# First pair's rows selected on chip by TensorE products, and two weight units asked for behind the second pair's gather

## The chip, the cores and the metric

The kernel runs on one core of one Trainium2 chip. The metric is the device time of one execution in microseconds (us). The kernel before takes 1109.01 us, the median of three runs (1107.18 to 1111.49). Besides its compute engines (PE for matrix products, DVE, ACT and POOL) the core has SP, which here only issues transfers, and 16 DMA engines which all issuing engines share.

## The reference

It is a decoder trunk with two layers over 512 tokens of 1024 f32 values. The first layer mixes tokens by differential attention, the second by multi-head latent attention. Each is followed by a mixture of experts: 4 groups of 8 experts, of which a token uses the best two of its best group. All weights are f32. What matters here:

```python
def hier_moe(h, w_group, b_group, w_router, b_router, w1, w3, w2):
    ...
    g_idx = jnp.argmax(g_prob + b_group.astype(jnp.float32), axis=-1)
    ...
    _, e_idx = lax.top_k(e_prob + b_router.astype(jnp.float32)[g_idx], TOP_K)
    ...
        a = jnp.einsum('nd,edf->nef', t, w1[g])
        b = jnp.einsum('nd,edf->nef', t, w3[g])
        hid = jax.nn.silu(a) * b * combine[:, g, :, None]
        out = out + jnp.einsum('nef,efd->nd', hid, w2[g])
```

with w1 and w3 of shape (1024, 256) and w2 of shape (256, 1024) for each of the 32 experts.

## The kernel before

The change lies in the experts of both layers. The 32 experts are taken as 16 pairs, expert n with expert n + 16. A pair's tile has 128 rows: the first 64 are tokens of expert n, the last 64 tokens of expert n + 16. Tokens beyond 64 of one expert go to overflow tiles, behind the ninth pair.

**Routing.** `gate(l)` on DVE finds the two experts of each token (`OH`, one-hot, and `Mb`, their sum). `route(l)` on PE (line 918) counts, by products with a triangle and with ones, the rank of each token within its expert. DVE turns the ranks into places in the pair's tile (`place`, lines 2040 to 2044) and those into the one-hot `hot_place` (line 2047). PE multiplies it with `hot_token` (line 936), which gives, for all 16 pairs at once, the token number of each place. DVE writes these to `idx` (line 2052).

**Rows of a pair.** The normed rows `XN` were written to HBM (`xn_d`) before. POOL waits for `idx` and gathers the rows of pair 0 into `xg[0]` and of pair 1 into `xg[1]`, by two indirect transfers (line 2515, semaphores gath0 and gath1). PE turns `xg[0]` (`turn_first_pair`, line 969), and ACT and DVE scale it into `xgT` (`modulate_first_pair`). While nothing is to be done, PE runs `keep_busy`, products on a unit matrix whose result nobody reads (line 741).

**A step.** `expert_step(l, n)` on PE: `into_hidden` for w1 (semaphore a) and for w3 (b), both at line 979; the turn of the next pair's rows (951) and of the hidden values (986); `out_of_hidden` for w2 (y, line 994). In step 0 the place table of all pairs is made between b and the turn (`weigh_places`, line 945), from one-hots that DVE made in `weigh(l)` (lines 2077 to 2095). DVE reads it in `tables_out`, and POOL scatters the results of each pair to `y_d` (line 2529).

**The weights.** A step needs six units of 1 MB: two of w1, two of w3, two of w2. SP asks for units in a fixed order (line 565). There are 22 places for units: six in `ring`, six each in the regions RQK and AHS, two in `X` (18 and 19, "the residual's place"), two in `spare`. The first 22 units of a layer are asked for as their places come free; two of these, number 8 and 9 (w3 of pair 1), go into `X`, and SP asks for them last, behind this wait:

```python
for b in range(2):
    sp.wait_ge(sem(f"gath{b}"), 16 * (PAIRS // 2 * l + 1))
first_units(l, 18, 19)
experts(l, BANKS, (4, 5))
```

Each further unit, from number 22 on, waits for the step that read its place 22 units before: those for w1 places for a, for w3 places b, for w2 places y. SP handles all in order, so all of them also stand behind the wait above.

Of the kernel before, what the change touches and what calls it, by code (L numbers as in the profile page):

```python
# [30 lines left out]
P = 128  # L31
# [36 lines left out]
BANKS = 3  # L68
SLOTS = BANKS * RING + 4
# [160 lines left out]
def build(nc, A, out):  # L230
    stack = ExitStack()
    with stack:
# [6 lines left out]

        def sem(name):  # L240
# [160 lines left out]
        half_of, place, over_cap, raw = scratch(PS, 2 * T), scratch(PS, 2 * T), scratch(PS, 2 * T), scratch(PS, 2 * T)  # L401
# [12 lines left out]
        hotp = view(GM, 0, 2 * T, P)  # L414

# [82 lines left out]
        def _(sp):  # L498
# [89 lines left out]
            for l in range(2):  # L588
# [16 lines left out]
                for b in range(2):  # L605
                    sp.wait_ge(sem(f"gath{b}"), 16 * (PAIRS // 2 * l + 1))
# [44 lines left out]
        def _(pe):  # L651
# [266 lines left out]
            def route(l):  # L918

                pe.wait_ge(sem("el"), 2 * (l + 1))  # L920
                keep_busy(3, 16)
                pe.wait_ge(sem("M"), l + 1)
                ranks = PB[6][:, 0:T * E].rearrange("p (t e) -> p t e", t=T)
                mm(PB[6][:, 0:T * E], trib[:, :], Mb.rearrange("p t e -> p (t e)"), start=True, stop=False)
# [30 lines left out]
            def turn_pair(l, n, chunks):  # L955

                b, m = n % 2, PAIRS * l + n
                pe.wait_ge(sem(f"gath{b}"), 16 * (PAIRS // 2 * l + n // 2 + 1))
# [54 lines left out]
            def expert_step(l, n):  # L1013
# [13 lines left out]
                if n == 0:  # L1027
                    pe.wait_ge(sem("xhA"), l + 1)
                    pe.wait_ge(sem("xhD"), l + 1)
# [11 lines left out]
                if n == 0:  # L1041
                    weigh_places(l)
# [15 lines left out]
                out_of_hidden(w, tiles).then_inc(sem("y"), 1)  # L1058

# [239 lines left out]
        def _(act):  # L1299
# [329 lines left out]
            def modulate_first_pair(l):  # L1629

                for h, (turned, done) in enumerate((("xh", "xhA"), ("xgt", "xA"))):
# [93 lines left out]
        def _(dve):  # L1725
# [262 lines left out]
            def gate(l):  # L1988
# [46 lines left out]
                tt(hot_step, oh[:, :, 0:PAIRS], oh[:, :, PAIRS:], ALU.add)  # L2035
                link(red(half_of, oh[:, :, PAIRS:], AX.X, ALU.add))
                tt(hot_token, hot_step, over(token_v.rearrange("p t k -> p (t k)"), 2, PAIRS), ALU.mult)
                link(ts(half_of, half_of, float(CAP), None, ALU.mult))
# [3 lines left out]
                ts(over_cap, raw, CAP - 0.5, 1024.0, ALU.is_ge, ALU.mult)  # L2042
                link(tt(place, raw, half_of, ALU.add))
                link(tt(place, place, over_cap, ALU.add))
                for h in range(2):
                    js = slice(T * h, T * h + T)
                    tt(hot_place[:, js], over(place[:, js], 2, P), over(iota_p, 1, T), ALU.is_equal).then_inc(sem("hotp"), 1)
                dve.wait_ge(sem("rank"), 2 * l + 2)
                link(v.tensor_copy(cnt, PB[7][:, T * E:(T + 1) * E]))
                v.tensor_copy(rank, PB[6][:, 0:T * E].rearrange("p (t e) -> p t e", t=T))  # L2050
                dve.wait_ge(sem("tab"), 2 * l + 1)
                ts(idx[:, 0:PAIRS], PB[2][:, 0:PAIRS], -1.0, float(S), ALU.mult, ALU.add).then_inc(sem("idx"), 1)
# [3 lines left out]
                link(red(extra, cmp, AX.X, ALU.add))  # L2056
                cur = extra
# [15 lines left out]
            def weigh(l):  # L2073
# [13 lines left out]

                link(tt(slots, over(slotf, 2, NPAIR), over(starts, 1, 2 * T), ALU.is_ge))
# [8 lines left out]
            def tables_out(l):  # L2097

                dve.wait_ge(sem("tab"), 2 * l + 2)
# [534 lines left out]
```

## Time and profile before

| | |
|---|---|
| time of the profiled execution | 1109.18 us |
| its span | 1107.4 us |
| granted TensorE clock, mean | 0.988 |
| PE busy | 1041.3 us, 94% of the span |
| DVE busy | 611.5 us, 55% |
| ACT busy | 328.6 us, 30% |
| POOL busy | 92.0 us, 8% |
| HBM read | 320.90 MB |
| chain that ended last, by engine | PE 75%, DMA 10%, DVE 5%, SP's queue 4% |
| experts of the first layer, first product to last step's last product | 350.38 to 551.2 us |
| experts of the second layer, the first product | 862.95 us |

The span is that of the profiled execution, which took 1.8 us more than its span. Times in the rows are in microseconds from the span's start. A busy share of PE does not say that PE sets the time: the products of `keep_busy` count too. What a change in one stage is worth is read from the waits of that stage and of those behind it.

### The profile page before, as it was taken

Reading aid. Unit: us, or ns where it says so; the run is one execution under the profiler, and the core shown is the slowest. Engines: PE = TensorE matmul, PEld = TensorE weight load, DVE = VectorE, ACT = ScalarE, POOL = GpSimd, SP = SyncE. Lnnn points to the kernel's source line nnn. Section 1 sums busy time; section 2 is a strip of 40 time slices with the busy share of each in tenths; the row PEclk is TensorE's granted clock in tenths of the full one; section 3 lists DMA queues with packets and bytes.
Section 4 is the critical chain, followed back from the end, with each engine's and each line's share of the span. In section 5 each row is a group of like instructions: output and inputs, shape, how many; then the busy total and the mean of one; then the engine's idle time right before and its main releaser. Section 6 shows DMA issues by size and latency. Waiting matters only on the chain.

```text
span 1107.4 us, 15314 instructions
## 1 busy us (share of the span) xinstructions
PE 1041.3 (94%) x5662; PEld 630.0 (57%) x5662; DVE 611.5 (55%) x1479; ACT 328.6 (30%) x891; POOL 92.0 (8%) x129
## 2 busy tenths in 40 slices
PE   6999999999998999898889999999998899979986
PEld 5444444555458666565556566565456666646652
DVE  6799989898647422222246577877236622222224
ACT  4321111874231211111114555666122211111110
POOL 1000000000011212121000000000000111101100
PEclk8999999999998999999999999999999999999999
DMA  9939967947578999999996400401837899999998
GB/s 366 404 132 395 393 264 297 386 171 297 235 291 328 401 419 418 418 418 419 417 394 269 166 1 1 189 2 50 367 115 305 346 419 419 417 397 417 419 416 351
DMA packets 66814, 341.44 MB, mean 308 GB/s; under 512 B 11110, under 2 KB 11366, under 8 KB 36400
## 3 DMA queue, kind: packets, MB, share of 16 engines
q1 hardware_dynamic: 49952, 297.68, 66.7%
q0 software_dynamic: 15120, 37.63, 8.9%
q10 hardware_dynamic: 1664, 5.09, 1.2%
q8 instruction: 48, 0.79, 0.3%
q14 instruction: 30, 0.25, 0.1%
HBM read 320.90 MB, written 37.24 MB: 323 GB/s over the span
## 4 chain that ended last, share of the span: by engine, by line
PE 75%; DMA 10%; DVE 5%; SPq 4%; ACT 3%; issue 3%; ACTq 0%; DVEq 0%; POOLq 0%
PE PP L979 16%; PE PP L732 12%; PE PP L842 10%; PE PP L994 8%; DMA AHS<-in_moe_w 5%; SPq L565 4%; PE PP L754 3%; PE PP L1199 3%; PE PP L1165 2%; PE PP L1203 2%; DMA AHS<-y_d 2%; PE PP L802 2%; PE PP L705 2%; PE PP L791 2%; PE PP L951 1%
## 5 line engine op out<-in xcount | busy, mean ns | idle before, releaser
L732 PE MATMUL PP<-ring,AHS 128*128 128x512 f32 x320 | 139.9, 592 | 0.0
L2148 DVE TENSOR_TENSOR PS<-PS,PP 128x256 f32<-128x256 f32 x33 | 13.9, 421 | 193.2 <-PE PP L979 183.7
L842 PE MATMUL PP<-ring,AHS 128*128 128x512 f32 x256 | 112.2, 594 | 0.0
L732 PEld LDWEIGHTS PP<-ring,AHS 128*128 128x128 f32 x320 | 59.7, 190 | 69.8 <-issue 69.8
L2155 DVE SCALAR_TENSOR_TENSOR PS<-PP,small,GF 128x512 f32<-128x512 f32 x66 | 46.5, 747 | 95.8 <-PE PP L994 85.4
L842 PEld LDWEIGHTS PP<-ring,AHS 128*128 128x128 f32 x256 | 47.8, 190 | 56.9 <-issue 56.9
L1642 ACT ACTIVATE PS<-PP 128x256 f32<-128x256 f32 x33 | 12.6, 383 | 216.5 <-PE PP L979 186.8
L979 PE MATMUL PP<-RQK,RV 128*64 128x256 f32 x640 | 71.9, 379 | 2.7 <-issue 2.7
L979 PE MATMUL PP<-AHS,RV 128*64 128x256 f32 (+1 forms) x592 | 68.7, 380 | 2.3 <-DVE RV L2142 1.3
L979 PE MATMUL PP<-ring,RV 128*64 128x256 f32 (+1 forms) x528 | 64.3, 391 | 4.1 <-issue 2.1
L979 PEld LDWEIGHTS PP<-RQK,RV 128*64 128x64 f32 x640 | 54.7, 137 | 21.9 <-issue 8.9
L979 PEld LDWEIGHTS PP<-AHS,RV 128*64 128x64 f32 (+1 forms) x592 | 51.1, 138 | 19.5 <-issue 6.6
L979 PEld LDWEIGHTS PP<-ring,RV 128*64 128x64 f32 (+1 forms) x528 | 49.1, 144 | 20.7 <-issue 8.7
L2529 POOL DMA_INDIRECT y_d<-PS,row x31 | 31.8, 1027 | 329.0 <-DVE PS L2155 286.1
L1872 DVE TENSOR_REDUCE small<-PP 128x2 f32<-128x256 f32 (+3 forms) x64 | 52.5, 822 | 8.5 <-PE PP L757 8.4
L2124 DVE TENSOR_SCALAR RV<-PP,small 128x128 f32<-128x128 f32 x124 | 42.4, 406 | 24.1 <-PE PP L951 23.2
L1748 DVE SCALAR_TENSOR_TENSOR ring<-ring,PS 128x1024 f32<-128x1024 f32 x44 | 51.8, 1221 | 4.3 <-DMA ring<-in_ada_t 3.9
L1646 ACT ACTIVATE PS<-PP 128x256 f32<-128x256 f32 x33 | 12.6, 383 | 136.4 <-PE PP L986 136.4
L1618 ACT ACTIVATE RV<-PP,small 128x128 f32<-128x128 f32 x124 | 46.6, 456 | 3.5 <-PE PP L951 3.5
L741 PE MATMUL PP<-ident 128*128 128x128 f32 x280 | 40.3, 307 | 4.4 <-POOL GM L2435 2.2
L1429 ACT ACTIVATE AHS<-PP,small 128x256 f32<-128x256 f32 (+3 forms) x82 | 41.1, 510 | 11.0 <-DVE small L1872 10.8
L1748 DVE SCALAR_TENSOR_TENSOR AHS<-AHS,PS 128x1024 f32<-128x1024 f32 x36 | 42.5, 1222 | 1.5 <-DMA AHS<-in_ada_t 1.0
(366 smaller groups left out, 1711.4 us busy)
## 6 DMA issues: line engine op xcount, KB each, us to landing
AHS<-in_moe_w SPq DMA_DIRECT2D x54, 1024.0 KB, 23.0
RQK<-in_moe_w SPq DMA_DIRECT2D x52, 1024.0 KB
ring<-in_moe_w SPq DMA_DIRECT2D x49, 1024.0 KB, 21.9
ring<-in_ada_t SPq DMA_DIRECT2D x22, 1024.0 KB, 21.1
AHS<-in_ada_t SPq DMA_DIRECT2D x18, 1024.0 KB
spare<-in_moe_w SPq DMA_DIRECT2D x16, 1024.0 KB, 13.6
X<-in_moe_w SPq DMA_DIRECT2D x16, 1024.0 KB
ring<-in_da_w_qkv SPq DMA_DIRECT2D x10, 1024.0 KB, 13.3
```

What stands on the lines that cost most here:

```text
L565: sp.dma_start(unit(slot), (w1, w3, w2)[k // 2][l][n + PAIRS * (k % 2)]).then_inc(s_w[slot], 16)
L732: last = mm(PB[qkv_bank(n)][:, :], HT[:, c, t * P:(t + 1) * P], us[c // 4][:, (c % 4) * NH:(c % 4 + 1) * NH], start=c == 0, stop=c == C - 1)
L741: mm(PB[bank][:, 0:P], ident[:, :], ident[:, :], start=True, stop=True)
L842: last = mm(PB[2 * t + n][:, :], (OT, OTM)[l][:, k, t * P:(t + 1) * P], us[k // 2][:, (k % 2) * D + n * NH:(k % 2) * D + (n + 1) * NH], st ...
L979: last = mm(o[s0:s1, 0:FF], xgT[b][:, c, s0:s1], w(2 * m + e)[:, c * FF:(c + 1) * FF], start=c == 0, stop=c == C - 1)
L994: last = mm(PB[5 + m][s0:s1, :], hidT[:, c, s0:s1], w(4 + e)[:, c * D + m * NH:c * D + (m + 1) * NH], start=c == 0, stop=c == 1)
L1429: last = fn(dst, src, ACT.Exp, bias=nmx[:, b, a:a + 1], accum_out=total)
L1618: last = fn(xgT[b][:, c, :], PB[0][:, (c // 2) * P:(c // 2 + 1) * P], ACT.Identity, bias=MODC[:, l, 3 + V_SHIFT, c:c + 1], scale=GC[:, 2 * ...
L1748: last = stt(wt, wt, 1.0, condb, ALU.mult, ALU.mult, accum_out=MODC[:, l, w, 2 * q + c:2 * q + c + 1])
L1872: red(nmx[:, b], o, AX.X, ALU.max, negate=True).then_inc(sem("nm"), 1)
L2124: last = ts(xgT[b][:, c, :], PB[1][:, (c // 2) * P:(c // 2 + 1) * P], GC[:, 2 * l + 1, c:c + 1], MODC[:, l, 3 + V_SHIFT, c:c + 1], ALU.mul ...
L2155: last = stt(ysb[b][:, cols], PB[5 + m][:, :], weight, GF[:, cols], ALU.mult, ALU.mult)
```

## The change

For pair 0 alone the rows no longer come by a gather. DVE makes `take_first`, for each of the four tiles of 128 tokens a one-hot of 128 tokens by 128 places of the tile, in f32; PE multiplies each with that tile's `XN`, two halves of 512 columns by four tiles, and sums them in PSUM; ACT copies one half into `xg[0]`, DVE the other. To tell experts 16 to 31 apart, PE adds 1024 to their ranks by a product of ones with `eights`. The token numbers of all pairs are made behind the products of the rows, so `idx` comes after them. POOL then gathers pair 1 first. SP waits for gath1 alone. `weigh(l)` is split in three; its last part and `weigh_places` move behind the hidden values and behind w2's products of step 0.

```diff
@@ sync
-                for b in range(2):
-                    sp.wait_ge(sem(f"gath{b}"), 16 * (PAIRS // 2 * l + 1))
+                sp.wait_ge(sem("gath1"), gathered(l, 3))
                 first_units(l, 18, 19)
@@ tensor, route
-                keep_busy(3, 16)
+                keep_busy(3, 10)
+                for _ in range(6):
+                    mm(PB[3][:, 0:P], onesb[:, :], onesb[:, :], start=True, stop=True)
+                pe.wait_ge(sem("iota"), 2 * l + 1)
+                ranks = PB[6][:, 0:T * E].rearrange("p (t e) -> p t e", t=T)
+                mm(ranks, onesb[:, :], eights.unsqueeze(1).broadcast_to([P, T, E]), start=True, stop=False)
...
                 keep_busy(3, 5)
+                for _ in range(8):
+                    mm(PB[3][:, 0:P], onesb[:, :], onesb[:, :], start=True, stop=True)
                 for h in range(2):
-                    pe.wait_ge(sem("hotp"), 2 * l + h + 1)
+                    for t in range(T):
+                        if h == 0:
+                            pe.wait_ge(sem("hotp"), 6 * l + t + 1)
+                        last = mm(PB[3 + h][:, :], take_first[:, t], XN[:, t, h * NH:(h + 1) * NH], start=t == 0, stop=t == T - 1)
+                    last.then_inc(sem("tab"), 1)
+                for h in range(2):
+                    pe.wait_ge(sem("hotp"), 6 * l + T + h + 1)
                     for j in range(T * h, T * h + T):
                         last = mm(PB[2][:, 0:PAIRS], hot_place[:, j], hot_token[:, j], start=j == 0, stop=j == 2 * T - 1)
                 last.then_inc(sem("tab"), 1)
-                pe.wait_ge(sem("idx"), 2 * l + 1)
-                keep_busy(3, 16 if l else 22)
@@ tensor, turn_first_pair
-                pe.wait_ge(sem("gath0"), 16 * (PAIRS // 2 * l + 1))
...
+                    if c % (C // 2) == 0:
+                        pe.wait_ge(sem("xhD" if c else "xhA"), 2 * l + 1)
@@ scalar, modulate_first_pair
+                act.wait_ge(sem("tab"), 4 * l + 1)
+                fn(xg[0][:, 0:NH], PB[3][:, :], ACT.Identity).then_inc(sem("xhA"), 1)
@@ vector, gate
+                link(tt(first_at, raw, elsewhere, ALU.add))
+                for t in range(T):
+                    link(ts(take_first[:, t], iota_h, first_at[:, 2 * t:2 * t + 1], None, ALU.is_equal))
+                    stt(take_first[:, t], iota_h, first_at[:, 2 * t + 1:2 * t + 2], take_first[:, t],
+                        ALU.is_equal, ALU.add).then_inc(sem("hotp"), 1)
...
+                dve.wait_ge(sem("tab"), 4 * l + 2)
+                v.tensor_copy(xg[0][:, NH:D], PB[4][:, :]).then_inc(sem("xhD"), 1)
+                dve.wait_ge(sem("tab"), 4 * l + 3)
+                ts(idx[:, 0:PAIRS], PB[2][:, 0:PAIRS], -1.0, float(S), ALU.mult, ALU.add).then_inc(sem("idx"), 1)
@@ gpsimd
-                for n in range(2):
-                    gather_pair(n)
+                gather_pair(1)
```

On PE, in `route` and step 0 of the first layer, the order before is this (741 is `keep_busy`, 936 the token numbers, 969 the turn of pair 0, 979 products into the hidden values, 945 `weigh_places`):

```order
L741 MATMUL PP<-ident 128x128 x5
L936 MATMUL PP<-PS 128x16 x8
L741 MATMUL PP<-ident 128x128 x22
L969 MATMUL PP<-ident,RV 128x128 x8
L979 MATMUL PP<-AHS,RV 64x256 x16
L979 MATMUL PP<-RQK,RV 64x256 x16
L945 MATMUL PP<-PS,GM 128x64 x8
L951 MATMUL PP<-ident,RV 128x128 x5
```

and after it is this (746 and 943 keep PE busy, 948 selects rows, 953 makes the token numbers, 985 turns pair 0, 995 goes into and 1010 out of the hidden values, 960 is `weigh_places`):

```order
L746 MATMUL PP<-ident 128x128 x5
L943 MATMUL PP<-onesb 128x128 x8
L948 MATMUL PP<-RV,GM 128x512 x8
L953 MATMUL PP<-PS 128x16 x8
L985 MATMUL PP<-ident,RV 128x128 x8
L995 MATMUL PP<-AHS,RV 64x256 x16
L995 MATMUL PP<-RQK,RV 64x256 x16
L966 MATMUL PP<-ident,RV 128x128 x5
L1002 MATMUL PP<-ident,PS 128x128 x2
L966 MATMUL PP<-ident,RV 128x128 x3
L1010 MATMUL PP<-RQK,PS 64x512 x8
L960 MATMUL PP<-PS,GM 128x64 x8
```

The 22 idle products are gone, the 8 selecting products of 512 columns stand ahead of the token numbers, and `weigh_places` moved behind w2's products.

On DVE, at the end of `gate` of the first layer, the writing of `idx` stood behind two short copies (2047 makes `hot_place`):

```order
L2044 TENSOR_TENSOR PS<-PS 128x8 [waits s_dve]
L2047 TENSOR_TENSOR PS<-PS 128x512 [waits s_dve]
L2047 TENSOR_TENSOR PS<-PS 128x512
L2049 COPY PS<-PP 128x32 [waits s_rank]
L2050 COPY PS<-PP 128x128 [waits s_dve]
L2052 TENSOR_SCALAR idx<-PP 128x16 [waits s_tab]
```

and now it stands behind the copy of half of pair 0's rows, which itself waits for the second half of the selecting products:

```order
L2070 COPY PS<-PP 128x32 [waits s_rank]
L2071 SCALAR_TENSOR_TENSOR PS<-PS,PP 128x128 [waits s_dve]
L2073 TENSOR_TENSOR PS<-PS,small 128x128
L2074 TENSOR_REDUCE PS<-PS 128x32 [waits s_dve]
L2077 COPY RV<-PP 128x512 [waits s_tab,s_xd,s_dve]
L2079 TENSOR_SCALAR idx<-PP 128x16 [waits s_tab]
L2172 TENSOR_SCALAR RV<-PP,small 128x128 [waits s_xh,s_gf]
```

What moved is `idx`, for which POOL's gather of pair 1 waits, and behind that SP.

## Rows read from the trace of the kernel before

**Rows 1.** The page's slices of the span, DMA share in tenths

```profile
DMA  9939967947578999999996400401837899999998
```

**Rows 2.** Chain that ended last, in order of time: start us, us, what

```profile
340.17 1.29 DVE PS L2047 x2
...
357.51 1.93 PE PP L945 x16
...
517.65 29.84 DMA AHS<-in_moe_w
...
856.82 4.32 DMA RV<-xn_d,idx
...
1039.68 29.54 DMA AHS<-in_moe_w
```

**Rows 3.** Waits of PE, stretch 470 to 552 us: us in total, times, longest us

```profile
PE PP L979 <- issue: 4.1, 3, 2.1
...
PE PP L994 <- DMA ring<-in_moe_w: 1.1, 1, 1.1
...
PE PP L994 <- DMA AHS<-in_moe_w: 0.6, 1, 0.6
```

**Rows 4.** SP's queue in order of time: start us, us, line, operation

```profile
332.49 0.83 SPq L565 DMA_DIRECT2D AHS<-in_moe_w  x2
...
348.28 0.80 SPq L565 DMA_DIRECT2D X<-in_moe_w  x2
...
354.09 1.95 SPq L565 DMA_DIRECT2D AHS<-in_moe_w  x2
...
862.92 0.80 SPq L565 DMA_DIRECT2D X<-in_moe_w  x2
...
992.11 0.33 SPq L565 DMA_DIRECT2D ring<-in_moe_w  x1
```

**Rows 5.** Busy time by stretch: us, engines, PEclk, DMA share, GB/s

```profile
343.00:348.00 5.00, 5.00 (x32) 5.00 (x32) 3.44 (x16) 0.00 (x0) 2.07 (x2) 0.66 0.46 128
...
882.00:902.00 20.00, 19.30 (x144) 12.14 (x142) 5.84 (x16) 4.05 (x11) 3.24 (x4) 1.00 1.01 416
...
991.00:995.00 4.00, 1.73 (x11) 0.80 (x11) 1.47 (x3) 0.00 (x0) 0.73 (x1) 1.00 0.77 266
```

**Rows 6.** Timeline of the second layer: start us, us, engine, line

```profile
853.99 1.29 DVE L2047 TENSOR_TENSOR PS<-PS 128x512 f16<-128x512 f32 x2
...
855.64 0.17 DVE L2052 TENSOR_SCALAR idx<-PP 128x16 int32<-128x16 f32 x1
...
856.82 1.05 POOL L2515 DMA_INDIRECT RV<-xn_d,idx  x1 [13.73 <-issue]
...
858.18 1.03 POOL L2515 DMA_INDIRECT RV<-xn_d,idx  x1 [0.30 <-issue]
...
861.19 1.09 PE L969 MATMUL PP<-ident,RV 128*128 128x128 f32 x8 [1.49 <-DMA RV<-xn_d,idx]
...
862.95 3.67 PE L979 MATMUL PP<-AHS,RV 128*64 128x256 f32 x32 [0.66 <-DVE RV L2142]
```

**Rows 7.** Timeline of the first layer, the same places

```profile
342.04 6.80 PE L741 MATMUL PP<-ident 128*128 128x128 f32 x44 [0.27 <-DVE idx L2052]
...
344.35 1.02 POOL L2515 DMA_INDIRECT RV<-xn_d,idx  x1 [0.30 <-issue]
...
348.69 1.04 PE L969 MATMUL PP<-ident,RV 128*128 128x128 f32 x8
...
350.38 3.67 PE L979 MATMUL PP<-AHS,RV 128*64 128x256 f32 x32 [0.66 <-DVE RV L2142]
...
357.55 0.42 DVE L2148 TENSOR_TENSOR PS<-PS,PP 128x256 f32<-128x256 f32 x1 [0.70 <-PE PP L979]
```

**Rows 8.** Chain that ended last: products of 512 columns

```profile
309.56 13.82 PE PP L842 x32
```

**Rows 9.** DMA queues in the stretch 340 to 560 us: packets, MB, share

```profile
q0 software_dynamic: 4647, 8.15, 10.1%
```

More of the change, by code:

```diff
@@ L68 @@
 BANKS = 3
+HALF = 1024
 SLOTS = BANKS * RING + 4
@@ L238, in build, with gathered @@
         sems = {}
+        def gathered(l, n):
+            return 16 * ((PAIRS // 2 - 1 + n % 2) * l + (n - 1) // 2)
         def sem(name):
@@ L400, in build @@
         hot_step, hot_token = scratch(PS, 2 * T, PAIRS), scratch(PS, 2 * T, PAIRS, dt=F16)
-        half_of, place, over_cap, raw = scratch(PS, 2 * T), scratch(PS, 2 * T), scratch(PS, 2 * T), scratch(PS, 2 * T)
+        raw, iota_h, eights = scratch(PS, 2 * T), scratch(PS, P, dt=F16), scratch(PS, E, dt=BF16)
+        elsewhere, first_at = scratch(PS, 2 * T), scratch(PS, 2 * T)
         assert at[0] <= 2816
@@ L414, in build @@
         hotp = view(GM, 0, 2 * T, P)
+        take_first = view(GM, 0, T, P)
         def probabilities(i, a):
@@ L1058, in expert_step @@
                 out_of_hidden(w, tiles).then_inc(sem("y"), 1)
+                if n == 0:
+                    weigh_places(l)
             def overflow_tile(l, i, b):
@@ L2041, in gate @@
                 link(red(raw, slots, AX.X, ALU.add))
[L2042 to L2047, printed above, removed]
+                link(tt(first_at, raw, elsewhere, ALU.add))
[3 more added lines that the diff above has]
+                        ALU.is_equal, ALU.add).then_inc(sem("hotp"), 1)
+                for j in range(2 * T):
+                    last = ts(hot_place[:, j], iota_h, raw[:, j:j + 1], None, ALU.is_equal)
+                    if j % T == T - 1:
+                        last.then_inc(sem("hotp"), 1)
                 dve.wait_ge(sem("rank"), 2 * l + 2)
                 link(v.tensor_copy(cnt, PB[7][:, T * E:(T + 1) * E]))
-                v.tensor_copy(rank, PB[6][:, 0:T * E].rearrange("p (t e) -> p t e", t=T))
-                dve.wait_ge(sem("tab"), 2 * l + 1)
-                ts(idx[:, 0:PAIRS], PB[2][:, 0:PAIRS], -1.0, float(S), ALU.mult, ALU.add).then_inc(sem("idx"), 1)
+                stt(rank, over(eights, 1, T), -float(P), PB[6][:, 0:T * E].rearrange("p (t e) -> p t e", t=T), ALU.mult, ALU.add)
                 cmp = masked.rearrange("p t e -> p (t e)").rearrange("p (e k) -> p e k", k=LEVELS)
@@ L2071, in gate, with weights @@
                 link(red(slotf, slots, AX.X, ALU.add))
-            def weigh(l):
+            def weights(l):
                 slots = picked.rearrange("p t k e -> p (t k) e")
@@ L2086, in weigh @@
                 link(tt(Wt, Wt, over(s1, 2, 2), ALU.mult))
+            def weigh(l):
+                slots = picked.rearrange("p t k e -> p (t k) e")
                 link(tt(slots, over(slotf, 2, NPAIR), over(starts, 1, 2 * T), ALU.is_ge))
@@ L2165, in expert_step @@
                 if n == 0:
-                    tables_out(l)
+                    weigh(l)
                 if n < LAST:
@@ L2171, in expert_step @@
                     spread(hot_last, tokf[:, n:n + 1])
+                if n == 0:
+                    tables_out(l)
                 dve.wait_ge(sem("y"), m + 1)
@@ L2203, in experts @@
                 modulate_first_pair(l)
-                weigh(l)
+                overflow_places(l)
+                weights(l)
                 for n in range(BETWEEN):
@@ L2483, in tables @@
                            channel_multiplier=0, allow_small_or_imprecise_dtypes=True)
+                    g.iota(iota_h.rearrange("p (a b c d) -> p a b c d", a=2, b=2, c=8), [[HALF, 2], [32, 2], [1, 8], [8, 4]],
+                           base=0, channel_multiplier=0, allow_small_or_imprecise_dtypes=True)
+                    g.iota(eights, [[HALF // P, 2], [0, PAIRS]], base=0, channel_multiplier=0, allow_small_or_imprecise_dtypes=True)
                     g.iota(starts, [[P, NPAIR]], base=0, channel_multiplier=0, allow_small_or_imprecise_dtypes=True)
@@ L2520, in gather_pair @@
                     if n < PAIRS:
-                        b, q = n % 2, PAIRS // 2 * l + n // 2
+                        b = n % 2
                         wait(pool, sem("xgt"), PAIRS * l + n - 1 if n >= 2 else 0)
-                        wait(pool, sem(f"gath{b}"), 16 * q)
+                        wait(pool, sem(f"gath{b}"), gathered(l, n))
                         gather(xg[b], idx[:, n:n + 1], sem(f"gath{b}"))
```

22 lines of the change are left out of this document (11 added, 11 removed).

## The prediction

> **What bounds the kernel now.** I first read the slices of the page [rows 1]. The DMA engines work at nine tenths or more from about 360 us to the end of the first layer's experts, and again in the second layer's; at 882 to 902 us they move 416 GB/s with a share of 1.01 [rows 5], which I take as full. The chain of waits agrees: near the end of both layers' experts it goes through a weight unit that landed 29.84 and 29.54 us after it was asked for [rows 2]. That is a queue, not a latency: a unit of 1.05 MB takes 2.5 us at 416 GB/s. Then the waits of PE: from 470 us to the end of the first layer's experts they add up to 4.1 + 1.1 + 0.6 = 5.8 us, in five short pieces [rows 3]. So PE starts with 22 units in store, eats the store, and late in the experts gets its weights just as they land. From there on only one thing counts: when the DMA engines began their unbroken run, and how much they had to carry.
>
> Next, where that run begins. SP asks for the last units of the store at 332.49 us, then nothing until 348.28 us, when both gathers have landed; then two units for X, and the next at 354.09 us, when step 0 has freed a place [rows 4]. Between 343 and 348 us the DMA engines are at 0.46 and move 128 GB/s [rows 5], which is the two gathers. In the second layer SP goes on at 862.92 us [rows 4]. These two holes are the places where this change can give or cost time. PE's own start counts less, since its steps run ahead of the DMA engines only to wait later.
>
> **PE's start, in the second layer.** Before: `hot_place` runs from 853.99 us, `idx` is written at 855.64, the gathers are issued at 856.82 and 858.18, PE turns the rows from 861.19 and begins step 0 at 862.95 [rows 6].
>
> After: the small DVE work ahead is about the same, and the one-hot of the first tile (two operations of 128 columns, where `hot_place` takes 0.65 us for 512) should be ready near 854.1. PE then does 8 selecting products of 512 f32 columns. The row of the same shape has 32 instructions in 13.82 us [rows 8], and there one product is two instructions, so 8 products are 16 instructions: 16 x 13.82 / 32 = 6.9 us, to 861.0. The one-hots of the other tiles come faster than 0.86 us each and don't hold it up. Then the 8 narrow products for the token numbers: `weigh_places` takes 1.93 us for 8 of 64 f32 columns [rows 2], these have 16 columns of f16, so a quarter or less; I take 0.4 us, to 861.4. ACT's copy of the first half lies under the second half's products; DVE's copy of the second half, of the size of `hot_place`, so 0.7 us, lies under the narrow products and the first four turns. From the turn's start to step 0 it stays 862.95 - 861.19 = 1.76 us [rows 6]: 863.2. PE starts step 0 0.2 us later than before. The gather that goes and the products that come are worth the same.
>
> **PE's start, in the first layer.** The same chain stands 853.99 - 340.17 = 513.8 us earlier [rows 2, 6], so 349.4 us after the change, against 350.38 before: 1.0 us earlier. The gain is not the gather's: 44 idle instructions took 6.80 us from 342.04 and PE turned the rows only at 348.69 [rows 7], when SP shows that both gathers had landed by 348.28 [rows 4]. Either bound, +0.2 or -1.0 us, is under what PE later waits for its weights.
>
> **SP's release, the term that counts.** `idx` now waits for the selecting products, DVE's copy and the narrow products: 861.0 + 0.7 + 0.05, then the write of 0.17 [rows 6], so ready at 862.0 instead of 855.8. POOL issues 1.0 us after (as 855.81 to 856.82), at 863.0. Gather 1 is now the first, so it doesn't stand 1.4 us behind another. Its time to land I take from the first gather of this layer, 4.32 us from its issue [rows 2]; the bounds are 3.93 (344.35 to 348.28, first layer [rows 4, 7]) and 4.74 (858.18 to 862.92 [rows 4, 6]). SP is released at 863.0 + 4.4 = 867.4 in the second layer, 4.5 us later than 862.92, and at 867.4 - 513.8 = 353.6 in the first, 5.3 us later than 348.28. With the bounds: 4.1 to 4.9, and 4.9 to 5.7.
>
> The Trainium skill, page "DMA: Bandwidth & Descriptors", section "Anatomy of one DMA — SWDGE (gpsimd) path", fits such a DMA as 2.0 us plus its bytes over 436 GB/s. For the mean 0.26 MB that would be 2.6 us behind POOL's 1.05 us, 3.7 us in all. The row's 4.32 us is more, and I go by it; by the page each release would be 0.7 us earlier and the time about 1.4 us less.
>
> All this time the DMA engines have nothing but gather 1: the store is full, and unit 22, which could start on a place freed by a (about 353 and 867 us), stands in SP's queue behind the same wait. So the hole grows by the whole delay. What comes off: gather 2 is issued at about its old time, behind gather 1, and now runs in the hole. The gathers and scatters are 8.15 MB in 32 transfers, 10.1% of 220 us, so 0.7 us each [rows 9]: -0.7 us per layer.
>
> **Does the delay reach the end?** In the first layer I see no later hole, the share stays full to the end [rows 1], and PE already waits [rows 3]: +5.3 - 0.7 = +4.6 us, and PE's 1.0 us is only a longer wait. In the second layer there is an overflow tile; SP waits for it until 992.11 [rows 4] and the DMA engines run dry: 991 to 995 us move 266 GB/s [rows 5]. That lacks 4 x (416 - 266) / 416 = 1.4 us of work, which a later queue fills: +4.5 - 0.7 - 1.4 = +2.4 us. Bounds for a layer's passing on: nothing, if DMA has slack I don't see, to all of it, 4.6 + 3.8.
>
> **The other edits.** `weigh_places` (1.93 us) moves behind w2's products: PE has the same work in step 0, 0. Behind it stand `tables_out` and the first scatter, needed many microseconds later. DVE's places and weights now run after the first pair's scaling; DVE stood 0.70 us waiting before the hidden values of step 0 [rows 7] and moves the last part of `weigh` behind them, so I cost it at 0; without that cover it is some tenths in step 0, again under PE's later waits. Pair 1's rows are turned when both products into the hidden values are through, 349.4 + 2 x 3.67 = 356.7 us [rows 7], three microseconds after gather 1 lands. Units 8 and 9 (w3 of pair 1) are read a step later than those of pair 0, and land about 1 + 2 x 2.5 us behind SP's release, near 360, before step 1 has even begun. The shorter `keep_busy`, the product with `eights`, two iotas on POOL while it idles: 0.
>
> **Sum.** 1109.18 + 4.6 + 2.4 = 1116.2 us for an execution like the profiled one; that execution is 0.17 us above the median of the runs, so 1116.0.
>
> **Rivals.**
> 1. *PE's start decides.* If the DMA engines had at least 5 us in hand before the first step that waits for weights, the longer hole would cost nothing, and the steps would end -1.0 + 0.2 us from before: 1108.2, not slower. For it: PE is 94% busy, and the waits of 5.8 us are spread thin. Against it: there are such waits in the first layer, and the share is full before them. It decides only where the delay is smaller than that reserve, and a reserve and waits don't go together.
> 2. *Only one layer passes it on.* In the second layer PE waits less, and the dry stretch may swallow more than its own 1.4 us: 1109.0 + 4.6 = 1113.6.
> 4. *Faster.* It needs 5.5 us, and nothing in the profile has them: even selecting products at half their price would bring SP's release only 3.5 us forward, still later than before.
>
> **How the numbers follow.** Both layers pass the delay on, my forecast: 0.56, own range 1113.5 to 1118.5. One layer alone: 0.18. The clock: 0.12. PE's start: 0.09. Something faster: 0.05. A measurement of this kernel can tell about 0.5%, 5.5 us, from no change, so slower means above 1114.6: all of the clock case and most of the forecast, with a little of the second, 0.66. Within 0.5%: 0.29. The range goes from 1110.5, which leaves out PE's start, to 1119.
>
> **What would show it.** In the changed kernel's profile SP's units into X are asked for near 353.6 and 867.4 us, with the DMA engines all but idle from 343 us and 855 us; 16 instructions of the selecting products take 6.9 us; step 0 begins near 349.4 and 863.2; the waits of PE for weights in the last steps of the first layer grow from about 6 to 11 us. I am wrong if SP is released by 350 us, or if it is late and the last product of the first layer's experts still ends near 551 us.

## The result, and the profile after

The changed kernel takes 1115.47 us (median of 4 runs, 1115.2 to 1115.99), the kernel before 1108.91 (4 runs, 1107.18 to 1111.49): a ratio of 1.0061, interval 1.0045 to 1.0077. It is slower by 6.6 us; the forecast was 1116.0. The profiled execution took 1115.3 us, its span 1113.5, against 1107.4 before, so the traces below differ by 6.1 us.

The page's slices of the changed kernel, DMA share in tenths, to set beside [rows 1]:

```profile
DMA  9939977947586999999996400401847799999998
```

Thirteenth slice: 6 in place of 8. That slice holds the hole in which the DMA engines wait for SP. Its queue in the changed kernel (start us, us, line, operation), beside [rows 4]:

```profile
332.44 0.81 SPq L571 DMA_DIRECT2D AHS<-in_moe_w  x2
353.10 0.80 SPq L571 DMA_DIRECT2D X<-in_moe_w  x2
...
870.75 0.81 SPq L571 DMA_DIRECT2D X<-in_moe_w  x2
```

The stretches of [rows 5] in the changed kernel, with one more (us, engines, PEclk, DMA share, GB/s):

```profile
343.00:348.00 5.00, 5.00 (x23) 2.37 (x21) 1.61 (x7) 0.60 (x1) 0.00 (x0) 1.00 0.01 5
348.00:353.00 5.00, 4.56 (x41) 3.53 (x42) 4.58 (x23) 2.99 (x6) 2.12 (x2) 1.00 0.29 71
...
991.00:995.00 4.00, 2.69 (x7) 0.90 (x5) 1.27 (x2) 0.00 (x0) 0.00 (x0) 1.00 1.00 414
996.00:1007.00 11.00, 5.24 (x26) 3.31 (x28) 0.00 (x0) 0.00 (x0) 2.56 (x3) 0.54 1.01 415
```

SP's next units come 4.8 us later in the first layer (353.10 against 348.28), and ten microseconds go by with the DMA engines nearly idle: 5 GB/s, then 71. The clock is full where the selecting products run. At 991 to 995 us the dry stretch is gone (414 GB/s, 266 before). From 996 to 1007 PE is busy for only 5.24 of 11 us, which I had not forecast.

The changed kernel's timeline, both layers (start us, us, engine, line; 948 selects the rows, 953 makes the token numbers, 2079 writes `idx`, 2551 gathers, 995 goes into the hidden values), beside [rows 6, 7]:

```profile
340.29 7.13 PE L948 MATMUL PP<-RV,GM 128*128 128x512 f32 x16 [0.35 <-DVE GM L2063]
347.26 0.35 PE L953 MATMUL PP<-PS 128*128 128x16 f16 x8
348.16 0.17 DVE L2079 TENSOR_SCALAR idx<-PP 128x16 int32<-128x16 f32 x1
349.20 2.60 PE L995 MATMUL PP<-AHS,RV 128*64 128x256 f32 x22 [0.24 <-DVE RV L2172]
349.29 1.09 POOL L2551 DMA_INDIRECT RV<-xn_d,idx  x1 [19.65 <-PE PP L985]
...
864.71 0.17 DVE L2079 TENSOR_SCALAR idx<-PP 128x16 int32<-128x16 f32 x1
865.74 3.67 PE L995 MATMUL PP<-AHS,RV 128*64 128x256 f32 x32 [0.24 <-DVE RV L2172]
865.88 1.05 POOL L2551 DMA_INDIRECT RV<-xn_d,idx  x1 [20.19 <-PE PP L985]
```

From the first selecting product to the first narrow one is 347.26 - 340.29 = 6.97 us. Everything here is as it was forecast, within half a microsecond. The end of the first layer's experts, before and then after (start us, us, engine, line):

```profile
552.59 7.13 PE L979 MATMUL PP<-RQK,RV 128*64 128x256 f32 x64 [1.35 <-issue]
...
564.22 1.94 PE L1009 MATMUL PP<-RQK,PS 128*64 128x512 f32 x8 [0.55 <-DMA RQK<-in_moe_w]
...
567.66 3.70 PE L1084 MATMUL PP<-PS,RQK 128*128 128x512 f32 x8 [0.19 <-DVE PS L2155]
```

```profile
555.19 7.13 PE L995 MATMUL PP<-RQK,RV 128*64 128x256 f32 x64 [1.34 <-issue]
...
566.87 1.94 PE L1025 MATMUL PP<-RQK,PS 128*64 128x512 f32 x8 [0.56 <-DMA RQK<-in_moe_w]
...
570.31 1.12 PE L1100 MATMUL PP<-PS,RQK 128*128 128x512 f32 x2 [0.19 <-DVE PS L2185]
```

These rows also mend an error: the time table ahead of the prediction, and its last part, call 551.2 us the end of the first layer's experts. That is the end of w2 of the 15th step; the 16th begins at 552.59 and its w2 ends at 566.2. The right comparison is 566.2 against 568.8 us: +2.6.

PE's waits over the last steps of that layer, 470 to 569 us (us in total, times, longest), before:

```profile
PE PP L979 <- issue: 5.4, 4, 2.1
PE PP L1009 <- DMA RQK<-in_moe_w: 1.6, 2, 1.1
PE PP L994 <- DMA ring<-in_moe_w: 1.1, 1, 1.1
...
PE PP L994 <- DMA AHS<-in_moe_w: 0.6, 1, 0.6
...
PE PP L994 <- DMA spare<-in_moe_w: 0.5, 1, 0.5
```

and after:

```profile
PE PP L995 <- issue: 8.5, 6, 2.1
PE PP L1010 <- DMA ring<-in_moe_w: 1.7, 1, 1.7
PE PP L1010 <- DMA spare<-in_moe_w: 1.7, 1, 1.7
PE PP L1025 <- DMA RQK<-in_moe_w: 1.7, 2, 1.1
...
PE PP L1010 <- DMA RQK<-in_moe_w: 0.7, 1, 0.7
...
PE PP L1010 <- DMA AHS<-in_moe_w: 0.5, 1, 0.5
```

Sums: 9.2 and 14.8, so +5.6 us. PE started 1.2 us sooner, and lost 1.7 us less to a halved clock in this layer (3.4 before, 1.7 after, by slices of 2.5 us), so 5.6 - 1.2 - 1.7 = +2.7 us at the end: the DMA engines set the end, and what PE gained it spent waiting. I count the waits that the profile calls "issue" as waits for weights. They stand ahead of w1's or w3's products and grew with the others, but their releaser isn't shown.

What the DMA engines moved gives the same by another way (340 to 400 us; before, changed, then two kernels of the next section: before with SP held, and changed without SP's wait):

```profile
340.00:400.00 60.00, 56.50 (x432) 40.65 (x434) 29.27 (x90) 11.65 (x29) 10.73 (x10) 0.97 0.94 369
340.00:400.00 60.00, 57.99 (x408) 36.32 (x410) 31.61 (x103) 12.37 (x30) 9.76 (x9) 1.00 0.85 344
340.00:400.00 60.00, 56.48 (x434) 40.55 (x436) 29.31 (x90) 11.67 (x29) 10.72 (x10) 0.97 0.87 349
340.00:400.00 60.00, 57.91 (x409) 36.31 (x410) 31.70 (x103) 12.37 (x30) 9.73 (x9) 1.00 0.95 380
```

The changed kernel is 25 GB/s x 60 us = 1.5 MB behind the kernel before. Of these 0.31 MB are pair 0's gather, which it no longer carries (2.26 against 1.95 MB on the gathers' queue), so 1.2 MB of weights are missing, or 2.8 us at 416 GB/s; the layer ended 2.6 us later. By the same sum the held kernel is 1.2 MB or 2.9 us behind, and ended 3.1 later; the one without the wait is 0.66 + 0.31 = 0.97 MB or 2.3 us ahead, and ended 2.0 sooner.

Where the second layer's share went shows in the chain of waits behind its overflow tile (start us, us, what), before and then after:

```profile
988.30 3.71 PE PP L994 x8
...
992.04 1.42 DVE PS L2155 x2
993.46 0.81 issue
994.27 8.78 PE PP L979 x63
```

```profile
989.99 3.71 PE PP L1010 x8
...
993.73 1.42 DVE PS L2185 x2
995.15 6.61 issue
1001.76 1.51 PE PP L995 x5
```

A stall of 0.81 us in which PE waits for nothing that the profile shows has become 6.61. With DVE's part, PE stands 2.27 us before and 8.07 after. The page counts 5662 matmul records of PE before and 5624 after.

### The profile page after: what moved, and what is told of

Same layout as the page of the kernel before. It is cut to its first block, busy times and chain, and to the rows that moved or that the text cites. A ratio compares the mean times of both kernels' runs of the same rounds, so it can differ in the third digit from the quotient of the medians.

```text
span 1113.5 us, 15268 instructions
## 1 busy us (share of the span) xinstructions
PE 1042.9 (94%) x5624; PEld 620.0 (56%) x5624; DVE 616.2 (55%) x1503; ACT 330.3 (30%) x893; POOL 91.2 (8%) x131
## 4 chain that ended last, share of the span: by engine, by line
PE 72%; DMA 9%; DVE 8%; SPq 4%; ACT 4%; issue 4%; ACTq 0%; DVEq 0%; POOLq 0%
PE PP L995 17%; PE PP L737 10%; PE PP L847 10%; PE PP L1010 9%; SPq L571 4%; DMA ring<-in_ada_t 3%; DMA AHS<-in_moe_w 3%; PE PP L759 3%; PE PP L1215 3%; PE PP L1181 2%; PE PP L1219 2%; DMA AHS<-y_d 2%; PE PP L807 2%; PE PP L796 2%; PE PP L966 2%
## 5 line engine op out<-in xcount | busy, mean ns | idle before, releaser
L995 PE MATMUL PP<-ring,RV 128*64 128x256 f32 (+1 forms) x528 | 61.1, 379 | 4.5 <-issue 2.6
L995 PEld LDWEIGHTS PP<-ring,RV 128*64 128x64 f32 (+1 forms) x528 | 46.4, 139 | 20.8 <-issue 9.6
L1950 DVE TENSOR_TENSOR PS<-PP,GM 128x512 f32<-128x512 f32 x16 | 11.1, 691 | 51.0 <-PE PP L847 50.8
```

The source lines that it names most:

```text
L995: last = mm(o[s0:s1, 0:FF], xgT[b][:, c, s0:s1], w(2 * m + e)[:, c * FF:(c + 1) * FF], start=c == 0, stop=c == C - 1)
```

## Experiments: when SP is released

The theory is that of the prediction: what counts is when SP may ask for its next units, and not when PE starts. Three kernels test it.

**The changed kernel without SP's wait.** Edit:

```diff
-                sp.wait_ge(sem("gath1"), gathered(l, 3))
                 first_units(l, 18, 19)
```

> The changed kernel, but SP asks for the two units in X without waiting for a gather. Theory H (what costs is the time in which the DMA engines have nothing to carry before step 0 frees a place): the two units are carried in the hole, SP's next unit waits only for step 0's a at about 353 and 870 us, so the DMA engines are 5 us of work further on in each layer; time 1106 to 1109 us. Gather 1 still lands before 357 us. Rival P (what costs is the selecting products on TensorE's path): step 0 starts as in the changed kernel and the time stays at 1115 to 1116.

Measured: 1109.47 us (12 runs), ratio to before 1.0004 (0.9993 to 1.0014). That is half a microsecond above the range expected, and the wait alone is worth 6.0 us; with it gone the change costs nothing. SP asks at 341.49 us, and the last residual products of the first layer start at 565.7 in place of 570.3, and of 567.66 in the kernel before. The stall behind the overflow tile stays, at 8.43 us. So the even time is a sum: 2.0 us won in the first layer, and 3.2 lost from step 0 to the last residual products of the second (228.8 against 225.6 us), with smaller differences elsewhere.

**The kernel before, holding SP for one gather more.** Nothing else of the change is made.

```diff
                 for b in range(2):
-                    sp.wait_ge(sem(f"gath{b}"), 16 * (PAIRS // 2 * l + 1))
+                    sp.wait_ge(sem(f"gath{b}"), 16 * (PAIRS // 2 * l + 2 - b))
```

> The kernel before, but SP waits for the landing of the third gather (pair 2) too before it asks for the two units in X, near 355 us and 868 us; step 0 starts as in the kernel before. Theory H: SP's release is 5 to 7 us late in each layer with nothing else changed, time 1115 to 1120 us. Rival P: TensorE's path is that of the kernel before, time 1109 us within 2 us.

Measured: 1115.49 us (9 runs), ratio 1.0050 (1.0034 to 1.0066): most of the loss, with PE's instructions as they were. SP's queue:

```profile
353.55 0.81 SPq L565 DMA_DIRECT2D X<-in_moe_w  x2
...
871.11 0.80 SPq L565 DMA_DIRECT2D X<-in_moe_w  x2
```

In the first layer that is the release of the changed kernel, and the layer ends 3.1 us later than before (residual products at 570.79). In the second the likeness of 871.11 and 870.75 misleads. This kernel's gathers are issued there 4.8 us later than before (861.65 against 856.82), so its release is late by only 8.2 - 4.8 = 3.4 us of its own, where the changed kernel's is late by 5.2. From step 0 (867.68) to the last residual products it takes 227.7 us, 2.1 more than the 225.6 before. Another 1.6 us passed between the two layers' experts, where the granted clock was 0.76 from 704 to 711 us and 1.00 before; that is not SP's doing. So the late release is enough for 3.1 + 2.1 = 5.2 us, which is most of the loss, and by the first experiment it is also needed.

**The kernel before without SP's waits.**

```diff
-                for b in range(2):
-                    sp.wait_ge(sem(f"gath{b}"), 16 * (PAIRS // 2 * l + 1))
                 first_units(l, 18, 19)
```

> The kernel before, but SP asks for the two units in X without waiting for the gathers. Theory H: the gathers now share the DMA engines with 2 MB, pair 0's rows land 3 to 5 us later, step 0 and its a come as much later, and so does the unbroken run; 1112 to 1117 us. Rival Q (a wait for a gather is always loss): 1104 to 1107 us.

Measured: 1114.3 us (8 runs), ratio 1.0047 (1.003 to 1.0065). An earlier release is no gain there: the units go ahead of the gathers, PE waits for pair 0's rows, and step 0 starts at 352.8 us in place of 350.4 and at 870.4 in place of 863.0. Of the second delay only 1.9 us arise there: the kernel was already 5.6 us late ahead of its route (DVE's last normed tile at 846.04 against 840.48). In the changed kernel pair 0 needs no gather, so its SP can be let go. That is what the selecting products are good for.

## Experiments: the stall behind the overflow tile

Theory J held that something which PE needs for the next step has to come through full DMA engines; its rival was that the stall follows from the place in PE's program.

**Units asked for later.** The changed kernel, with three units of the 11th pair asked for behind the overflow tile, so that the DMA engines are nearly free there.

```diff
-                experts(l, BETWEEN + 1, (1, 3, 5))
                 with sp.If(0 < tails):
                     sp.wait_ge(sem(f"oy{l}"), tails)
                     sp.sem_inc(sem("turns"), 1)
+                experts(l, BETWEEN + 1, (1, 3, 5))
```

> The changed kernel, but three of the units of the eleventh pair are asked for behind the overflow tile instead of ahead of it, so that the DMA engines are idle when TensorE leaves the overflow tile of the second layer. Theory J (TensorE's stall of 8.07 us there is its code, which comes through the same full DMA engines): the stall falls to 2 to 3 us and the time to 1111 to 1114 us. Rival (the stall is not tied to the DMA engines' load, or the weights are what it waits for): the stall stays at 6 to 8 us or grows, time 1115 us or more.

Measured: 1120.39 us (6 runs), ratio 1.0101 (1.008 to 1.0121). At the stall's start the DMA engines were as free as planned (they fill again from about 996 us), and the stall stayed (stretch: us, engines, PEclk, DMA share, GB/s; then PE's timeline):

```profile
992.00:996.00 4.00, 2.08 (x5) 0.57 (x3) 1.47 (x3) 0.00 (x0) 0.00 (x0) 1.00 0.39 109
```

```profile
1002.53 1.98 PE L995 MATMUL PP<-spare,RV 128*64 128x256 f32 x8 [8.45 <-issue]
```

The kernel before with SP held has full DMA engines at that place, and the short stall:

```profile
992.00:996.00 4.00, 3.41 (x9) 1.64 (x10) 0.07 (x1) 0.59 (x2) 0.00 (x0) 1.00 1.02 426
```

```profile
998.19 0.65 issue
```

As the reason for the two lengths theory J fell: full DMA engines go with the short stall, and engines that are free as it begins don't shorten it. They were free only until about 996 us of a stall that lasts until 1002.5, so whether engines that stay free would shorten the long one is not shown.

**Fewer idle products in the kernel before.** 19 f32 products less over the two layers, which are 38 matmul instructions and as many weight loads, all idle work.

```diff
-                keep_busy(3, 16 if l else 22)
+                keep_busy(3, 10 if l else 9)
```

> The kernel before with fewer idle products while it waits for the first gather (9 for 22 in the first layer, 10 for 16 in the second), so that TensorE's program reaches the overflow tile of the second layer 76 instructions sooner, as in the changed kernel. Theory L: the stall there grows from 2.2 to about 8 us and the time to 1111 to 1115 us. Rival M: the stall stays at 2.2 us and the time at 1109 us or 1 us less, as step 0 of the first layer starts 1 us sooner.

Measured: 1112.11 us (12 runs), ratio 1.0028 (1.0013 to 1.0044). The stall is the long one, and 5.6 us longer. Not all of the loss comes from it: step 0 of the second layer starts at 864.35 in place of 862.95, with a granted clock of 0.62 from 844 to 853 us, and the steps behind the stall take 2.1 us less than before.

```profile
1000.64 3.68 PE L979 MATMUL PP<-spare,RV 128*64 128x256 f32 x16 [7.91 <-issue]
```

**More idle products in the changed kernel**, at the program's start, where PE waits for its first data anyway: 66 products in bf16 in place of 14 in f32 (28 matmul instructions), so 38 instructions more, and as many weight loads.

```diff
             pe.wait_ge(sem("const"), 2)
-            keep_busy(7, 14)
+            for _ in range(66):
+                mm(PB[7][:, 0:P], onesb[:, :], onesb[:, :], start=True, stop=True)
```

> The changed kernel with 14 idle f32 products at the very start (28 matrix instructions with as many weight loads) replaced by 66 idle bf16 ones (66 with as many), so that TensorE's program reaches the overflow tile of the second layer after as many instructions as in the kernel before. Theory L (the stall behind the overflow tile of the second layer, 8.07 to 8.45 us in three kernels with the change and 2.1 to 2.3 us in three without it, depends on where in TensorE's program the jump lands): the stall falls to about 2.2 us, and the time to 1111 to 1114 us, as then the late weights bind. Rival M (the stall comes with the change's own waits or buffers): it stays at 8 us and the time at 1115 to 1116 us.

Measured: 1116.88 us (6 runs), ratio 1.0057 (1.0035 to 1.0078). The stall is short again:

```profile
999.10 5.14 PE L995 MATMUL PP<-spare,RV 128*64 128x256 f32 x30 [2.10 <-DVE PS L2186]
```

But the time did not fall, as I had expected it to. From the end of the overflow tile's stall to the last residual products it is 1094.9 - 1001.8 = 93.1 us in the changed kernel and 1095.7 - 999.1 = 96.6 here. During the long stall the DMA engines go on filling the store (416 to 424 GB/s from 992 to 1000 us), and afterwards PE's waits for weights add up to 0.7 us; without it they are 4.9 us, "issue" counted with them. The two losses lie over each other.

**Both: more idle products, and no wait of SP.** The two edits together.

> Both edits at once: SP asks for the two units in X without waiting for a gather, and the 66 idle bf16 products at the start. Theories H and L: no hole of 5 us and no stall of 8 us, 1103 to 1106 us, below both kernels. Rival M: as without the products at the start, 1109 to 1110 us.

Measured: 1106.68 us (12 runs), ratio to before 0.9976 (0.9962 to 0.9989). That is faster than both kernels, by 2.7 us than the one before (1109.4 on the same chip) and by 8.8 than the changed one's 1115.47, and just above the range expected. Its stall:

```profile
991.36 3.67 PE L994 MATMUL PP<-spare,RV 128*64 128x256 f32 x32 [2.10 <-DVE PS L2185]
```

So the stall does cost 1109.47 - 1106.68 = 2.8 us where the weights are in time; the two were run on different chips, and their ratios to before, 1.0004 and 0.9976, give 3.1 us.

**How many idle products.** The changed kernel without SP's wait, with 38, 47 and 104 idle products in place of 66 (10, 19 and 76 matmul instructions more than the changed kernel has, and as many weight loads).

> The changed kernel without SP's wait for the gather, and with 38 idle bf16 products at the start of PE's program in place of the 14 idle f32 ones: 10 products (20 instructions of PE) more than there were. After 38 more products the stall of PE behind the overflow tile of the second layer was 2.1 us and without them 8.4 us. If the stall turns short from some count of instructions on, I expect 8 us here, since 10 is far from 38. If it goes with the place modulo something smaller, 2 us is as likely. Time 1109 us with the long stall, 1106 with the short one.

> As the kernel with 10 products more, but 19 (38 instructions of PE). Half way between the long stall (0 more) and the short one (38 more): no theory of mine says which; with the two neighbours it shows between which counts the turn lies. Time 1109 us with a stall near 8, 1106 with one near 2.

> As before, but 76 products (152 instructions of PE) more than the changed kernel, twice the count that made the stall short. Theory that only enough instructions ahead are wanted: the stall stays near 2.1 us and the time near 1106.7. Theory that the stall goes with the place in some block of the program: it may be near 8 again, and the time near 1109.5.

Measured, one run each: 1109.52, 1106.7 and 1112.18 us, the kernel before on the same chip 1108.8. All three have a short stall: 2.18, 2.22 and 2.11 us. My expectation of 8 us at 10 missed, and the long stall doesn't come back at 76. The kernel with 104 lost 2.5 us because its idle work outlasts the wait for the first data (step 0 at 351.8 us, 349.3 with 38); the other 3.0 us between it and the one with 47 go with three stretches of halved clock behind the first layer's experts, as in the one with 38. The one with 38 had the short stall and yet took 1109.5, for a reason of its own. PE stood 1.9 us in both it and its neighbour with 47, and then ran sixteen instructions at two speeds (38, then 47 products; timeline, then stretch):

```profile
977.99 5.38 PE L994 MATMUL PP<-ring,RV 128*128 128x256 f32 x16 [1.91 <-DVE RV L2154]
978.00:983.00 5.00, 5.00 (x16) 4.11 (x17) 0.00 (x0) 0.00 (x0) 0.33 (x1) 0.66 1.00 421
```

```profile
976.25 3.69 PE L994 MATMUL PP<-ring,RV 128*128 128x256 f32 x16 [1.90 <-DVE RV L2154]
976.30:981.30 5.00, 5.00 (x24) 4.41 (x25) 0.00 (x0) 0.00 (x0) 0.29 (x1) 1.00 1.03 432
```

```
kernel                           packet   tile's end  packet   next step
before                           981.0    992.0        997.5    994.3
before, SP held                  985.5    996.7       1001.5    998.8
changed, no wait, +38            979.5    989.2        995.0    991.4
changed, no wait, +19            981.0    989.0        994.5    991.2
changed, no wait, +10            991.0    992.4        998.0    994.6
changed, no wait, +76            978.5    995.2       1001.0    997.3
changed                          968.0    993.7        998.5   1001.8
changed, no wait                 963.5    989.2        995.0    997.6
changed, units later             968.5    994.1        999.5   1002.5
before, 38 fewer                 967.5    992.7        998.0   1000.6
changed, +38                     986.0    997.0       1002.0    999.1
before, no waits of SP           988.5    997.8       1003.5   1000.0
before, place table alone        982.0    991.2        996.0    993.4
```

In every kernel a packet comes 4.8 to 5.8 us behind the tile's end, where PE's program jumps. Where another had come within 17 us ahead of it, PE goes on without waiting for it; where none had, for 25 us, PE goes on 2.6 to 3.3 us after that packet. From this I infer that PE waits for a block of its own program, and that whether it has it already depends on where the jump lies in its block. No trace names what PE waits for. The last run puts the inference to a test between 0 and 10.

> The changed kernel without SP's wait, with 33 idle bf16 products at the start (5 products, 10 instructions of PE, more than the changed kernel has). The traces of the other kernels show on DMA queue q8 (instruction) one packet of 16 KB about every 12 to 17 us. Where the stall behind the overflow tile is short, one lies ahead of the overflow tile's end: with 10 products more 1.4 us ahead of it, with 19 more 8 us. Where it is long, none does, and the next comes 2.6 to 3.3 us before the stall ends. Theory: PE reads its program in blocks, and waits for the block behind the jump unless it has been asked for already. Then 5 products less than in the kernel with 10 push the asking back by 10 instructions, which the products of w2 there (16 instructions in 3.7 us) turn into some 2.3 us, so a stall between the two lengths, 3.5 to 5 us; or, if that place lies behind the jump, the long one of 8.4 us and no packet ahead of it. Rival, that the count of instructions alone makes it one of two lengths and nothing is waited for: 2.2 or 8.4 us with the packet anywhere.

Measured: 1111.1 us (one run; the kernel before on that chip 1109.22), and a stall of 8.47 us. No packet lies between 963.5 us and the tile's end at 991.5; the next comes at 997.0, 2.9 us before the next step at 999.9. That is the second outcome of the theory, the place behind the jump, and fits the table. The stall between the two lengths, which the theory gave as its first outcome, didn't come, and of the two outcomes that the rival allowed this is one too; what speaks against the rival is the place of the packet. The turn lies between 5 and 10 products.

## Experiment: the place table alone

The kernel before with only that part of the change: `weigh_places` behind w2's products of step 0, `weigh` split.

```diff
@@ tensor, step 0
-                if n == 0:
-                    weigh_places(l)
                 if n < LAST:
                     turn_pair(l, n + 1, range(5))
...
                 out_of_hidden(w, tiles).then_inc(sem("y"), 1)
+                if n == 0:
+                    weigh_places(l)
@@ vector
                 modulate_first_pair(l)
-                weigh(l)
+                weights(l)
...
+                if n == 0:
+                    weigh(l)
                 if n < LAST:
                     modulate_pair(l, n + 1)
...
+                if n == 0:
+                    tables_out(l)
```

> The kernel before with only the place table's move: its one-hots and weights are made behind the hidden values of step 0, its products stand behind those of w2. Forecast: 0 within 1 us, 1108 to 1110 us. Rival: DVE's work comes late and holds step 1, 1110 us or more.

Measured: 1107.68 us (12 runs), ratio 0.9975 (0.9963 to 0.9987). It is a little faster than I had it. Its profiled execution shows no place for the gain: it is the slowest of the 12 (1109.32), its span is 1107.6 us against 1107.4, and the stall 2.25 us. It stays open.

## Why the prediction was right, and where it was not

- **SP's release.** Forecast 353.6 and 867.4 us, or +5.3 and +4.5. Measured 353.10, +4.8. In the second layer all was 2.6 us later by then (DVE makes `Mb`, ahead of the route, at 851.47 before and 854.06 after), so 870.75 is 868.2 in the forecast's time, +5.2. Right; gather 1 took 4.9 us there to land, where I had 4.4, and 3.8 us in the first layer. The next gather was issued 1.4 us behind it in both, so that is not the reason, which stays open.
- **PE's start.** Forecast 349.4 and 863.2; measured 349.20 and 865.74 - 2.59 = 863.15. The 16 instructions took 6.97 us for 6.9. Right.
- **That this delay decides, not PE's start.** Right: without the wait the loss is gone, with the wait alone it is there. Rival 1 falls.
- **The first layer passes on +4.6 us.** Too much: +2.6, and 3.1 in the kernel with SP held. I took the DMA engines of before as working at full rate from 349 us on. Their share was full, their rate not (before, then after):

```profile
356.00:370.00 14.00, 13.76 (x110) 9.80 (x108) 8.73 (x22) 2.21 (x6) 2.56 (x2) 1.00 1.00 380
```

```profile
356.00:370.00 14.00, 13.76 (x108) 8.55 (x106) 11.62 (x32) 2.22 (x6) 2.56 (x2) 1.00 1.02 427
```

  In 14 us that is 47 GB/s or 0.66 MB, 1.6 us of the 2.0 that failed to arrive. So the term that was too large is the 5.3 us of hole, counted at the full rate on the side of before. Why before moved less there is not shown.
- **The second layer passes on +2.4 us.** The trace has 6.1 - 2.6 = +3.5 at the end of the span, and from `Mb` to the last residual products 240.9 against 237.0 us, +3.9. The dry stretch was absorbed, as forecast. But the sum by places is another: start +0.2, steps up to the overflow tile's end -1.0, stall +5.8 (8.07 against 2.27), steps behind it -1.1. The late weights hardly bind behind the stall, for the stall hides them. With the stall padded away they do: that kernel takes 240.5 us, +3.5, of which 0.8 lie ahead of step 0 (12.24 against 11.48 us; in a clock of 0.76 from 846 to 860 us DVE waits 0.58 us for the ranks) and 2.7 behind it, where the forecast had 2.4. So the mechanism held where nothing hides it. What the prediction put at nothing without a reason is the effect of the instructions taken out ("The shorter `keep_busy` ...: 0"): I did not look at how they shift the rest of PE's program. The two misses, -2.0 and +1.5 us, nearly cancel, and that the sum of 1116.0 came so near is luck.
- **The other edits cost 0.** The place table alone came out at 0.9975, within 3 us of nothing; not a loss.
- **Rival 3, the clock.** The granted clock was 1.00 from 343 to 348 us, 0.66 before. This rival fell. The Trainium skill, page "TensorE: Matmul & The Clock Gate", section "What's actually happening", says that activity releases the throttle, and the traces agree: from 340 to 356 us none of the nine kernels with the selecting products shows a fall, and four of the five without them do. The fifth, the place table alone, stays at 1.00 with the idle products of before, so the selecting products are not needed for a full clock there. The same rule agrees with the half clock that follows the long stall, 0.54 on the mean from 996 to 1007 us.
- **Rival 2** gave 1113.6 with one layer passing the delay on. The first layer's 2.6 us alone would have been 1111.8; both passed something on.

Shown by runs: the release is the cause of the loss; the stall changes with idle instructions more or less, in both kernels, whatever the DMA load; and where it is long, its end follows an instruction packet by 2.6 to 3.3 us. Only argued: that PE waits for that packet; how the two split the second layer's 3.9 us, since they don't add. Open: what exactly makes the chip ask for a block, and why the place table alone was not even.

## What to carry to other kernels

When a transfer is replaced by work on chip, look at what else waited for the old order: here it was the DMA queue, which had been released by a gather that now comes last. A wait that guards a shared resource should be placed for the new schedule, or taken out with what made it needed; here that turned 0.6% slower into even. Work taken out of a long program shifts all that stands behind it, and with it the places where the engine may wait for its own instructions, as I infer here. And two losses that both hold PE up may overlap, so take each away alone and both together before you price them.

## What was unexpected of the hardware

- PE's stall between the overflow tile and the next step has two lengths, 2.1 to 2.3 and 7.9 to 8.5 us, by whether an instruction packet of 16 KB came ahead of the jump. 5 idle products more at the program's start left it long, 10 made it short; 38 matmul instructions fewer in the kernel before made it long. Both lengths stood with full DMA engines (414 and 426 GB/s).
- In the first layer, without an overflow tile, the stall before the same step is 3.73 us after (461.33) and 3.70 before.
- A DMA share of 1.00 went with 380 GB/s in one stretch and 1.02 with 427 in the same stretch of the other kernel. The share alone doesn't tell the rate.
- After PE had stood 1.9 us, the clock was halved for a while in one execution (1.7 us lost) and not in another, with the same instructions around it.
